# Raw rows turned for the router among the mixer's matmuls, and the last expert's down product on its own buffers with one root for both norms

## What is computed

```python
x = x + token_mixer(rmsnorm(x, norm_mix_g), ...)      # ends in m @ w_out, 1024 x 1024
h = rmsnorm(x, norm_ffn_g)
pg = softmax(h @ w_router_group)                       # 4 groups, best one taken
pe = softmax(h @ w_router_expert[best group])          # 8 experts in it, best two taken
x = x + sum over the two experts e of w_e * ((silu(h @ w_e_gate[e]) * (h @ w_e_up[e])) @ w_e_down[e])
x = rmsnorm(x, norm_final_g)                           # end of the first block
u = rms_norm(x, a_norm_g_2) @ a_w_in_2                 # start of the second block
```

## Time and profile before

| | us |
|---|---|
| median of 3 runs (lowest, highest) | 1975.03 (1970.85, 1975.04) |
| the profiled execution | 1973.54 |
| its span | 1971.7 |
| PE busy | 1825.6 (93%) |
| DVE busy | 1200.0 (61%) |
| ACT busy | 1000.5 (51%) |
| last matmul of the mixer to first of the experts | 615.7 to 660.5 |
| last down product's end to the first turning for the second block | 1193.9 to 1232.5 |

### The profile page before, as it was taken

The page is one execution under the profiler, slowest core; times in us unless marked ns, Lnnn a source line. Parts: engine busy times, 40 slices in busy tenths (PEclk is TensorE's granted clock), DMA queues, the critical chain, the costliest instruction groups (busy, mean ns, idle before and its releaser), DMA issues.

```text
span 1971.7 us, 23827 instructions
## 1 busy us (share of the span) xinstructions
PE 1825.6 (93%) x8926; PEld 1494.4 (76%) x8926; DVE 1200.0 (61%) x1642; ACT 1000.5 (51%) x1328; POOL 335.0 (17%) x191
## 2 busy tenths in 40 slices
PE   7999999999998699999999981979999998999898
PEld 6888878888787577777777770868778787878467
DVE  3452444545553899999999975661638643327453
ACT  4222244444412689898989873444243222438331
POOL 0000000000000255555555540110001000000000
PEclk9999999999999799999999995989999999999799
DMA  6755357343147499999999954222022332212001
GB/s 144 102 93 89 107 79 70 67 56 61 43 177 287 151 404 407 402 403 404 402 400 405 401 218 165 97 86 86 22 86 86 126 110 80 71 61 91 20 1 65
DMA packets 129364, 326.49 MB, mean 166 GB/s; under 512 B 8448, under 2 KB 84992, under 8 KB 121088
## 3 DMA queue, kind: packets, MB, share of 16 engines
q1 hardware_dynamic: 123408, 315.85, 49.4%
q0 software_dynamic: 5440, 8.93, 1.4%
q10 hardware_dynamic: 432, 0.56, 0.1%
HBM read 319.02 MB, written 15.21 MB: 170 GB/s over the span
## 4 chain that ended last, share of the span: by engine, by line
PE 59%; DVE 23%; issue 12%; ACT 5%; DMA 1%; DVEq 0%; SPq 0%; POOL 0%; POOLq 0%; ACTq 0%
PE bank L1318 15%; PE bank L1320 15%; PE bank L1319 15%; DVE down_lo L2174 5%; DVE gate_lo L2174 5%; DVE up_lo L2174 4%; PE bank L1400 2%; PE bank L1390 2%; DVE ys L2209 2%; PE bank L1485 2%; PE bank L1819 1%; ACT w_hi L849 1%; PE bank L1734 1%; DVE xs L2193 1%; PE bank L1818 1%
## 5 line engine op out<-in xcount | busy, mean ns | idle before, releaser
L1847 DVE TENSOR_TENSOR w_lo<-w_raw,w_hi 128x2048 fp32r<-128x2048 f32 (+2 forms) x83 | 179.5, 2164 | 340.0 <-ACT w_hi L849 339.9
L849 ACT ACTIVATE w_hi<-w_raw 128x2048 fp32r<-128x2048 f32 (+3 forms) x139 | 182.2, 1332 | 281.2 <-PE bank L1320 82.2
L1318 PE MATMUL bank<-h1T_hi,w_hi 128*128 128x512 f32 x456 | 183.4, 402 | 0.0
L1320 PE MATMUL bank<-h1T_hi,w_lo 128*128 128x512 f32 x456 | 179.3, 393 | 0.0
L1319 PE MATMUL bank<-h1T_lo,w_hi 128*128 128x512 f32 x456 | 178.7, 392 | 0.0
L776 POOL COPY put_row<-table 64x1 int32 (+1 forms) x32 | 121.0, 3781 | 180.6 <-DVE ys L2209 180.6
L2174 DVE TENSOR_TENSOR gate_lo<-gate,gate_hi 128x2048 fp32r<-128x2048 f32 x64 | 145.9, 2282 | 0.0
L2174 DVE TENSOR_TENSOR up_lo<-up,up_hi 128x2048 fp32r<-128x2048 f32 x64 | 143.5, 2283 | 0.8 <-ACT up_hi L849 0.8
L2174 DVE TENSOR_TENSOR down_lo<-down,down_hi 128x2048 fp32r<-128x2048 f32 x64 | 143.3, 2276 | 0.5 <-ACT down_hi L849 0.5
L849 ACT ACTIVATE gate_hi<-gate 128x2048 fp32r<-128x2048 f32 x64 | 122.4, 1914 | 8.2 <-DVE slot_r L2148 8.2
L849 ACT ACTIVATE up_hi<-up 128x2048 fp32r<-128x2048 f32 x64 | 119.1, 1921 | 0.0
(11 more groups left out here) (471 smaller groups left out, 4364.2 us busy)
## 6 DMA issues: line engine op xcount, KB each, us to landing
gate<-in_w_e_gate SPq DMA_DIRECT2D x32, 2048.0 KB, 12.1
up<-in_w_e_up SPq DMA_DIRECT2D x32, 2048.0 KB, 14.2
down<-in_w_e_down SPq DMA_DIRECT2D x32, 2048.0 KB, 15.7
w_raw<-in_w_in SPq DMA_DIRECT2D x24, 1024.0 KB, 9.1
w_raw<-in_a_w_in SPq DMA_DIRECT2D x20, 1024.0 KB, 5.2
w_raw<-in_w_in SPq DMA_DIRECT2D x16, 512.0 KB, 9.3
w_raw<-in_a_w_out SPq DMA_DIRECT2D x8, 1024.0 KB, 5.0
w_raw<-in_c_w_in SPq DMA_DIRECT2D x6, 1024.0 KB, 5.4
```

What stands on the lines that cost most here:

```text
L849: return nc.scalar.activation(out, in_, ACT.Copy, scale=scale)
L1318: pe.matmul(out, sh, mh, start=start, stop=False)
L1320: return pe.matmul(out, sl, mh, start=False, stop=stop)
L1847: V.tensor_tensor(ring_view(w_lo, n), ring_view(raw, n), ring_view(w_hi, n).bitcast(F32), ALU.subtract)\
```

## The change

1. `token_wide` gets a hook behind each finished token tile, and opens its banks one by one. The rows x of the mixer's first half are turned without norm or gain (`turn_x1`, 16 transpositions) between the two slices of the second half; the second half's are turned tile by tile, one tile late, and `logits_of(tt)` follows two tiles late. `h2T` moves to other memory and is laid out by token tile.
2. The router's gain goes into its weights once (`router_scaled`), 1/rms into the evicted logits. The rows get their gain on DVE beside the matmuls (`gained`) and their 1/rms from ACT at the end. A root on a spare element loads ACT's table early (`mark`).
3. `g_ffn` is loaded before the mixer's slices. The loads for expert 1 are parted: down at the mixer's end, up after the logits, gate after the stores of the rows.
4. After the expert loop the sums of expert 30 are made among the gate product of expert 31, and expert 31's sums stand ahead of expert 30's down product. Expert 31 gets `down_hi_last`, `hxs_last` and banks 3 and 5 of its own.
5. The second block's first three slices are loaded and the first one split before `moe_done`; `gfin` is loaded while the routing ends.
6. Both norms share one root on eight columns: the second mean square is taken from the sums, since r² = 1/var gives var2 = (ssq2/D + EPS·var)/var, and rstd2·r = rsqrt(ssq2/D + EPS·var).

```diff
-            for n in range(2):
-                token_wide("mix_out", n, 512, [(mixT_hi, mixT_lo, 0), (mixT_hi, mixT_lo, 4)], chunk_taken("att_out"))
+            def turn_x1(h, tt):
+                until_taken(pe, ("mix_out", h, tt))
+                transposes(("h2T", h, tt), [(x1_tok[:, tt, (4 * h + c) * P:(4 * h + c + 1) * P], P) for c in range(4)])
+            def logits_of(tt):
+                for h in range(2):
+                    until_taken(pe, ("h2T", h, tt))
+                for c in range(KC):
+                    ins = pe.matmul(out[:, tt * 36:(tt + 1) * 36], h2T[:, tt, c, :], w_router[:, c, :], start=c == 0, stop=c == KC - 1)
+            def after_mix(tt):
+                if tt >= 1:
+                    turn_x1(1, tt - 1)
+                if tt == 2:
+                    pe.wait_ge(sem("router_scaled"), 1)
+                if tt >= 2:
+                    logits_of(tt - 2)
+            token_wide("mix_out", 0, 512, mix_terms, chunk_taken("att_out"))
+            token_wide("mix_out", 1, 512, mix_terms, before={1: turn_first}, after=after_mix)
+            turn_x1(1, TT - 1)
+            logits_of(TT - 2)
+            logits_of(TT - 1).then_inc(results, 1)
...
-                V.scalar_tensor_tensor(out=h2_tok[:, tt, :], in0=x1_tok[:, tt, :], scalar=rstd[:, tt:tt + 1], in1=g_ffn[:, :],
-                                       op0=ALU.mult, op1=ALU.mult).then_inc(sem("h2_rows"), 1)
+                mix_add(1, tt)
+                gained(1, tt)
...
+                copy(h2_tok[:, tt, :], h2g[:, tt, :], rstd[:, tt:tt + 1]).then_inc(sem("h2_rows"), 1)
...
-            gate_product(last, 1)
-            sums(expert(last, -1))
+            gate_among(last, 1, turn_next=False)
             up_both(last, 1)
+            sums(last)
             down_both(expert(last, -1), 0)
-            sums(last)
-            down_both(last, 1)
+            pe.wait_ge(hx_lo_made, NE)
+            for f in range(FC):
...
+                        ins = pe.matmul(bank[(3, 5)[a]][:, :], hxs_last[:, f, :], w[:, f, a * 512:(a + 1) * 512],
...
+            sp.wait_ge(up_done, NE)
+            load_slice(slices1)
+            load_slice(slices1 + 1)
+            sp.wait_ge(down_done, NE - 1)
+            load_slice(slices1 + 2)
...
-            rsqrt(TT, D, 2 * TT)
-            step(V.tensor_copy(r_fin[:, :], rstd[:, 0:TT]))
-            step(V.tensor_tensor(ssum[:, 0:TT], ssq[:, TT:2 * TT], r_fin[:, :], ALU.mult))
-            step(V.tensor_tensor(ssum[:, 0:TT], ssum[:, 0:TT], r_fin[:, :], ALU.mult))
-            rsqrt(TT, D, 0, ssum)
-            diagonals(r_fin[:, :])
+            step(V.tensor_scalar(var[:, 0:TT], ssq[:, 0:TT], 1.0 / D, EPS, ALU.mult, ALU.add))
+            step(V.tensor_scalar(ssum[:, 0:TT], ssq[:, TT:2 * TT], 1.0 / D, None, ALU.mult))
+            V.scalar_tensor_tensor(out=var[:, TT:2 * TT], in0=var[:, 0:TT], scalar=EPS, in1=ssum[:, 0:TT],
+                                   op0=ALU.mult, op1=ALU.add).then_inc(var_made, 1)
+            newton_steps(2 * TT)
+            diagonals(TT)
```

## The result

The changed kernel took 1953.83 us (median of four runs, 1952.4 to 1955.12) against 1972.94 (1970.67 to 1975.04) for the kernel before in the same job: a ratio of 0.9899, 95% interval 0.988 to 0.9917. I had forecast 1951, with a range of 1945 to 1959. Repeated later (the run *after_again*), it took 1952.2 against 1973.36, ratio 0.9893 (0.9877 to 0.991). So 19 to 21 us were saved, where my sum had 24.3. The forecast started from 1975.03, the median of the three runs that I had; with the fourth run the median of before is 1972.94, and the same sum would have given 1948.6. So the 2.8 us between 1951 and 1953.83 understate the miss in what is saved, 5.2 us.

A forecast was written before the change was run, and what follows sets the result against it. PE was taken as the bound over most of the span, DVE's work plus ACT's copy as the loop's period. 11.1 + 7.0 + 1.7 + 1.8 + 2.7 = 24.3 us off 1975.03 gave 1950.7, stated as 1951; range 1945 to 1959.

The forecast's parts named there:

- Router, 11.1: Before the loop: diagonals and norm wait go, transpositions come in, logits at 626.2 instead of 637.5; 11.1 us saved.
- rival (b): Behind the mixer's last matmul, transpositions mixed with narrow matmuls lose 2.4 GHz; 5 us less saved, 1956; chance 0.06.
- The stored rows: Before the first gather: loads and row stores issued from 626.4 are through at 637, landed some 2 us later.
- The tie at POOL's clearing stores: Before the first gather: second clearing store through at 640 to 642, table at about 641.4; loss 0 to 1, taken as 0.
- The loop: no change: Expert loop: instructions inside stay as they are, same 16.2 us period; an earlier start reaches the end in full.
- Rival (c): Expert loop: loads come later than the 1.85 us margin, every period waits for DMA; 1981 at 1 us each; chance 0.02.
- Behind the loop, 7.0: Loop's end to `moe_done`: expert 31's down ends 7.9 us sooner, less 0.9 for expert 30's scatter; 7.0 saved.
- The pause for `u_sb`: Before expert 31's sums: PE waits some 4 us for ACT's copy, going on at 1174.4, 1.9 later than before.
- The split ... is done under the wait for the scatters: Before `moe_done`: DVE's 2.28 us split moves from behind the last square into waiting time; part of the 2.7 saved.
- From `moe_done` to the turning, 6.2: Three terms: `gfin`'s load off the first pair 1.7, second pair's wait 1.8, table load and one root's round 2.7.
- signs of being wrong: POOL waiting for clearing stores or stored rows, loop DMA waits, expert 31's `put` waiting for a scatter, clock 0.5 among turnings.
- rival (a): Loop's end: expert 30's scatter lands late, expert 31's `put` waits, costing 4 to 5 us; 18 saved, 1957; chance 0.14.

The follow-up runs named there:

- split_late: Changed kernel with DVE's split of the next stage's first slice moved from behind expert 31's row sums to behind `moe_done`; 1953.97 us, ratio 0.9901.
- router_only: Kernel before with only the router's part of the change, the end of the loop as before; 1962.45 us against 1973.19, ratio 0.9952.
- router_twice: Changed kernel with each tile's eight narrow router products done twice, same result; 1963.99 us in a single run, against 1972.46 for before.
- fill_pause: Changed kernel with 40 idle transpositions put into PE's 4.84 us pause before expert 31's sums; 1949.95 us, ratio to before 0.9879.
- kept_warm: Changed kernel with ACT's loop-end work reordered, DVE's split behind `moe_done`, `gfin` loaded at loop's end, idle transpositions at three places; 1945.62 us, ratio 0.9857.
- warm_gfin_early: kept_warm with `gfin`'s load back where the changed kernel has it, behind the first gathers' table; 1943.24 us against 1972.69, ratio 0.9856.

## Why the forecast came out 3 to 5 us too large

**Router, 11.1; measured 10.2, and 0.4 lost behind it.** No gap on PE, and up to the logits nothing late on DVE or ACT: the mechanism was right. Where the clock held, the step is worth 44.9 - 33.8 = 11.1, the forecast to the tenth; by my own terms it was 637.55 - 626.2 less a tenth, 11.25, so the last tenth is luck. Where the clock fell it is 10.2. That is rival (b), with 0.7 instead of my 5. I had blamed the mixture with transpositions; the rows point to the narrow matmuls, since more of them made it worse and transpositions alone held the clock.

One term here was sized wrongly, and the profile of the changed kernel hides it. The stored rows landed at 642.0, not at 639: ACT had made the last of them only at 629.65, and its store, issued at 630.06 with expert 1's gate load right behind it, took 12.0 us. The table was ready at 642.1, so nothing was lost. But in the eight later profiles of the changed kernel and its variants that have the single router product, POOL waited for these rows; where the clock had held, its copy of row numbers began 1.2 to 1.3 us behind the table's last cast instead of 0.32, here in after_again (last cast at 643.21, last store landed at 644.16):

```profile
644.39 0.18 POOL L782 COPY get_row<-table 64x1 int32<-64x1 int32 x1 [9.73 <-DMA h_dram<-h_tok]
```

So where the clock held, the table was 0.9 to 1.0 us too early for its rows. The tie at POOL's clearing stores cost nothing that the profiles show. The first gather took 4.3 us instead of 3.5, beside expert 1's gate load, which landed at 647.2 and not at 643. Of the 0.6 to 1.9 by which gate 0 started later behind the table, the start of the loop gave most back, and 0.4 stayed (514.45 to 514.87).

**The loop: no change**, as said. 506.3 and 506.2 us; the only DVE wait is again that for ACT's copy. Rival (c) is out.

**Behind the loop, 7.0; measured 5.0.** Two sizes and one step failed:
- The pause for `u_sb` was seen rightly (4.84 us; "some 4 us"), and its end at 1164.47, or 1174.42 on the old scale, is the 1174.4 of the text. The sums behind it took 3.13 us, not 2.3, since the clock had fallen, and down 30 ended 1.0 later than forecast: expert 31's down ends 6.8 us sooner, not 7.9.
- The scatter of expert 30 cost 0.5, not 0.9.
- "The split ... is done under the wait for the scatters" is the step that failed. I looked only for free time on DVE. Its cover was there, but it took POOL's copy with it, 1.34 us on the path; split_late shows it.

7.9 - 1.1 - 0.5 - 1.3 = 5.0. Of these 5.0 us 3.2 depend on before having had the low clock there; it did in both looks, and not in router_only's same code. The forecast took it from the one profile of before, so that it was near is partly luck.

**From `moe_done` to the turning, 6.2; measured 6.8.** First pair 2.25 for 1.7, the pairs 1.64 for 1.8, one root and the earlier table load 2.93 for 2.7. The table load in the trace was 1.28 us at its new place as well:

```profile
1178.29 1.28 ACT L1163 ACT_TABLE_LOAD   x1
1179.58 0.20 ACT L1163 ACTIVATE mark<-const 128x1 f32<-128x1 f32 x1
```

**Not in the sum:** the last turning took 0.56 longer (9.89 to 10.45), because PE starts it at 0.50 and the clock rose later into it. Over the profiles it takes 9.7 to 10.8 without help and 7.92 when PE has idle transpositions ahead of it.

So 24.3 - 0.9 - 0.4 - 2.0 + 0.6 - 0.6 = 21.0, the profiled 21.1. Most of what was missing is PE's clock at three places (0.9, 1.1 and 0.6) and one copy on POOL (1.3).

**The signs.** Of what I had named as signs of being wrong, three came, each small: a clock of 0.50 behind the turnings, expert 31's `put` waiting for the scatter ahead of it (the mechanism of rival (a); 0.5 us of the wait counted, and my sum had allowed 0.9), and, in later profiles, POOL waiting for the stored rows. No rival came at its full price, and the number lies in the range because each was small and the last stage gave 0.6 more than forecast.

## What to carry to other kernels

When work is moved into an engine's idle time, ask not only whether that engine is free but who shares a port with it: a split with two SBUF operands on DVE stopped a 0.18 us copy on POOL for 1.3 us, at the one place where that copy was the path. A mean of 3.78 us for a copy of 64 numbers on the page of before was the hint. Find what an engine does first when it comes back from a wait; ACT's 0.6 us copy behind a 1.9 us one cost PE 2.7 us. Compare traces by intervals between marks: the program's start alone differed by 5 us between executions, more than most terms of this sum.

## What the runs showed of the hardware

- PE's granted clock fell from 1.00 to 0.50 while PE was busy without a pause with matmuls of 36 columns (after); with twice as many the last row took 11.79 us instead of 7.3 (router_twice).
- A POOL copy of 64 int32 takes 0.18 us alone, 1.29 to 1.98 us when it begins beside a DVE operation with two SBUF inputs, and 4.03 us beside two in a row.
- Transpositions kept the clock at 1.00 over 4.5 us (fill_pause), and raised it from 0.50 ahead of the last turning, which then took 7.41 us instead of 9.2 to 10.2 (kept_warm):

```profile
1200.33 6.02 PE L1593 MATMUL bank<-const,x2g_tok 128*128 128x128 f32 x40 [24.17 <-DVE x2g_tok L2363]
1207.88 7.41 PE L1441 MATMUL bank<-diag,x2g_tok 128*128 128x128 f32 x64 [1.53 <-DVE diag L1971]
```

- A pause of 2.96 us left the clock up in router_only, and one of 2.94 us was followed by the low clock in both looks at before; in warm_gfin_early pauses of 1.09 and 1.52 us, with eight short transpositions between, were followed by 3.4 us at the low clock. A clock saved at one place was once lost at the next, for a reason that no run here settles.
